# Dealing the expert slots over the SBUF partitions: neighbouring slots of each 32 stand four partitions apart

## The reference, cut to what matters

```python
def hier_moe(x, w_rg, w_re, w_g, w_u, w_d):
    ...
    ids = g_idx[:, None] * E_PER_GROUP + top_i.astype(jnp.int32)
    wts = (g_w * top_w).astype(x.dtype)
    return expert_dispatch(t, ids, wts, w_g, w_u, w_d).reshape(shp)
# for each expert e and the tokens xb that chose it:
    hb = jax.nn.silu(xb @ w_gate[e]) * (xb @ w_up[e])
    return (hb @ w_down[e]) * wb[:, None]
```

```
layer 0: 26 22 62 31 36 31 48 66 31 26 24 22 18 31 13 17 47 49 28 50 51 53 40 32 36 48 37 43 34 21 34 45
layer 1: 23 12 31 16 15 23 16 30 81 57 65 86 45 24 88 28 38 54 39 33 26 66 41 29 28 18 26 15 21 31 35 12
```

## Time and profile before

| | us |
|---|---|
| Median of 3 runs | 1980.47 |
| Lowest and highest run | 1979.82, 1981.99 |
| Span of the profiled execution, first to last instruction | 1975.5 |
| Median less span | 5.0 |

### The profile page before, as it was taken

How to read it: one execution, slowest core, us unless ns; L and a number is a source line. 1 busy time by engine, 2 the same in 40 slices (tenths; PEclk the granted TensorE clock), 3 DMA queues, 4 the chain that set the end, 5 groups by cost and what they waited for, 6 DMA issues and landing times.

```text
span 1975.5 us, 32588 instructions
## 1 busy us (share of the span) xinstructions
PE 1654.4 (84%) x12810; PEld 790.5 (40%) x12810; DVE 643.1 (33%) x1305; ACT 330.3 (17%) x752; POOL 216.5 (11%) x356
## 2 busy tenths in 40 slices
PE   6999888888889787887778879998968788778885
PEld 3444355554445322322223347764442222223232
DVE  3213467777612500000000068984160000000005
ACT  2000244434402100000000020004020000000001
POOL 1001122223200100000000012000020000000000
PEclk9999889988889799999998979999979999999997
DMA  9999378989963799999999989804169999999995
GB/s 373 324 369 347 142 278 311 338 327 349 367 239 125 290 420 427 416 427 424 427 410 429 422 295 302 283 10 171 43 239 425 426 415 428 425 427 427 425 422 202
DMA packets 99924, 659.09 MB, mean 334 GB/s; under 512 B 15147, under 2 KB 15148, under 8 KB 69706
## 3 DMA queue, kind: packets, MB, share of 16 engines
q1 hardware_dynamic: 70906, 569.76, 72.5%
q0 software_dynamic: 28896, 87.65, 12.0%
HBM read 643.08 MB, written 96.53 MB: 374 GB/s over the span
## 4 chain that ended last, share of the span: by engine, by line
PE 54%; DMA 34%; DVE 6%; issue 3%; ACT 2%; SPq 1%; POOL 0%; DVEq 0%; POOLq 0%; ACTq 0%
DMA ring<-in 33%; PE ps L2059 14%; PE ps L1706 9%; PE ps L2014 7%; PE ps L2222 6%; PE ps L1665 4%; PE ps L1828 2%; PE ps L2243 2%; PE ps L2079 1%; PE ps L1768 1%; DMA ring<-y_rows 1%; PE ps L1893 1%; PE ps L1744 1%; PE ps L1813 1%; DVE ring L1185 1%
## 5 line engine op out<-in xcount | busy, mean ns | idle before, releaser
L2059 PE MATMUL ps<-ring,big 128*32 128x512 f32 (+1 forms) x2688 | 476.9, 652 | 139.0 <-DMA ring<-in 133.0
L2059 PEld LDWEIGHTS ps<-ring,big 128*32 128x32 f32 (+1 forms) x2688 | 150.9, 132 | 460.6 <-issue 390.6
L1382 DVE TENSOR_TENSOR big<-big,ps 128x512 f32<-128x512 f32 x32 | 22.0, 688 | 828.7 <-PE ps L2059 783.3
L2079 PE MATMUL ps<-ring,big 128*32 128x512 f32 (+1 forms) x928 | 212.3, 594 | 17.0 <-ACT big L748 12.3
L748 ACT ACTIVATE big<-ps 128x512 f32<-128x512 f32 (+4 forms) x136 | 74.4, 548 | 739.7 <-PE ps L1665 415.2
L1706 PE MATMUL ps<-ring,act_t 128*128 128x512 f32 (+1 forms) x480 | 189.8, 594 | 0.6 <-DMA ring<-in 0.6
L2014 PE MATMUL ps<-ring,big 128*128 128x512 f32 (+1 forms) x288 | 123.0, 609 | 5.7 <-ACT big L1085 4.8
L2222 PE MATMUL ps<-act_t,ring 128*128 128x288 f32 x512 | 124.4, 406 | 0.0
L1706 PEld LDWEIGHTS ps<-ring,act_t 128*128 128x128 f32 (+1 forms) x480 | 78.0, 179 | 97.2 <-issue 96.2
L2079 PE MATMUL ps<-act_t,big 128*32 128x512 f32 (+1 forms) x416 | 99.0, 594 | 14.8 <-ACT big L748 11.5
L2222 PEld LDWEIGHTS ps<-act_t,ring 128*128 128x128 f32 x512 | 97.2, 190 | 26.8
(11 more groups left out here) (292 smaller groups left out, 1616.7 us busy)
## 6 DMA issues: line engine op xcount, KB each, us to landing
ring<-in SPq DMA_DIRECT2D x180, 2048.0 KB, 21.4
out<-in SPq DMA_DIRECT2D x16, 4080.0 KB
ring<-in SPq DMA_DIRECT2D x128, 256.0 KB, 8.2
ring<-in POOLq DMA_DIRECT2D x128, 256.0 KB, 8.2
act_t<-in SPq DMA_DIRECT2D x16, 2048.0 KB
ring<-in SPq DMA_DIRECT2D x28, 1024.0 KB, 9.3
ring<-in SPq DMA_DIRECT2D x24, 512.0 KB, 4.9
ring<-in POOLq DMA_DIRECT2D x24, 512.0 KB, 4.7
```

What stands on the lines that cost most here:

```text
L2059: ins = mm(ps[half, i, :], XgT[:, par_, k, half], slot(eslots(w)[i], 8)[:, k, :], start=(k == 0), stop=(k == KC - 1))
L2079: ins = mm(ps[half, 5 + h, :], hbT[:, k, half], down_weights(w, odd)[:, k, h * 512:(h + 1) * 512], start=(k == 0), stop=(k == 3))
```

## The change

The constants get two new tensors, `slot_at` (128 columns) and `rank_at` (64 columns), 192 columns or 96 KB more in `cst`. Partition m of a block holds no longer slot m, but slot 32*(m//32) + 8*(m%4) + (m%32)//4: slots stay in their group of 32 partitions, and there slots 0 to 7 stand on partitions 0, 4, 8, ... 28, slots 8 to 15 on 1, 5, ... 29, and so on. The two comparisons that make the one-hots read the new constants. The gathers, scatters, matmuls and waits are those of before, in number, shape and order, with other indices in them.

```diff
@@ -108,6 +108,10 @@
     c["count_up"] = np.broadcast_to(np.arange(P, dtype=f), (P, P)).astype(f)
+    m = np.arange(P)
+    slot_at = 32 * (m // 32) + 8 * (m % 4) + m % 32 // 4
+    c["slot_at"] = np.broadcast_to(slot_at.astype(f), (P, P)).astype(f)
+    c["rank_at"] = np.broadcast_to(1 + slot_at[0:HB].astype(f), (P, HB)).astype(f)
@@ -1440,7 +1444,7 @@
             V.tensor_tensor(unit0, rank0.unsqueeze(3).broadcast_to((P, NT, 2, HB)),
-                            C("count_up")[:, 1:HB + 1].unsqueeze(1).unsqueeze(1).broadcast_to((P, NT, 2, HB)),
+                            C("rank_at").unsqueeze(1).unsqueeze(1).broadcast_to((P, NT, 2, HB)),
                             ALU.is_equal).then_inc(r_table, 1)
@@ -1506,7 +1510,7 @@
             V.tensor_tensor(in_block, lo.unsqueeze(2).broadcast_to((P, NS, P)),
-                            C("count_up").unsqueeze(1).broadcast_to((P, NS, P)), ALU.is_equal).then_inc(r_table, 1)
+                            C("slot_at").unsqueeze(1).broadcast_to((P, NS, P)), ALU.is_equal).then_inc(r_table, 1)
```

## The result

| | before | changed |
|---|---|---|
| Median, us | 1980.74 (4 runs, 1979.82 to 1981.99) | 1970.82 (4 runs, 1968.66 to 1974.18) |
| Ratio, 95% interval | | 0.9946 (0.9932 to 0.9960) |
| Time and span of the profiled execution, us | span 1975.5 | 1970.49, span 1968.3 |

The direction is the forecast's, the size is not. Of the changed kernel the time and the span of one and the same execution are known: 2.2 us lie between them, not the 5.0 us taken for before. If it is 2.2 us before the change too, the profiled execution of before was about 2.8 us quicker than the median it was set against. The forecast does not hang on that: 1980.5 less 5.7 us is 1974.8 either way.

What follows compares the result with a forecast made beforehand. Weight loads keep the DMA queues full in the experts' stretches, so the engine with most token rows binds, with PE a fifth spare. 7.3 - 0.4 - 1.0 - 0.2 = 5.7 us less, giving 1974.8 us; range 1971.2 to 1979.5.

Steps and rivals of the forecast that it cites:

- the 0.153 us priced from bytes and rate: Gathers and scatters: a 4 KB token row costs its DMA engine 4096 B / 26.8 GB/s = 0.153 us.
- theory G: Follow-up, experts over both halves: the block-by-block sum of heaviest counts matters, not the heaviest total; about 4 us under the change.
- theory E: Follow-up, gathers: neighbouring descriptors on one engine cost, not its row count; half dealing brings half the gain or less.
- The 5.2 us of layer 0: Experts of layer 0: heaviest engine has 17 fewer rows, in gathers and scatters, 34 x 0.153 = 5.2 us saved.
- the 2.1 us of layer 1: Experts of layer 1: 7 fewer rows counted in gathers and 7 in scatters, 14 x 0.153 = 2.1 us saved.
- engines nearly level: Experts' stretches: the slowest of several close engines is later than one alone; 0.5 us a layer, 1.0 us lost.
- the small packets: Gathers and scatters: where the engine lost a row it gets a very small packet; 0.4 us lost, ends 0 to 0.8.
- 0.2 for the constants: Start, ahead of the first weight load: 96 KB more at 429 GB/s costs 0.2 us on the path.
- Runs scatter by 1 us: Range of the forecast: 1 us of scatter moves its low end from 1972.2 to 1971.2 us.
- 1 (only part arrives): Experts' stretches: the loop issue, landing, PE holds the heavy engine; half the gain, 1977.0 to 1978 us; chance 0.11.
- 2 (the change does not do it): Indirect transfers shared among engines otherwise than inferred, so only the constants count; 1980.7 us; chance 0.08.
- 3 (the eighth engine is slow): Experts' stretches: the eighth engine, slower by itself, gets more rows; 11.3 us more, 1991.9 us; chance 0.05.

Runs made afterwards that it cites:

- experiment 8: Changed kernel with each expert's slots spread over both halves of the partitions, matmuls in four column groups of 32; 1971.71 us (0.9967 of before), again 1975.54 us (0.9985).
- seventh experiment: Kernel before, with the gathers of blocks 1 to 15 in layer 1 moving no row (out of bounds); 1969.24 us against 1978.06, ratio 0.9952.
- layer 1 only: Changed kernel with slots dealt in layer 1 alone, layer 0 as before; 1979.22 us against 1978.50 before, ratio 0.9997.
- two apart: Changed kernel with half the dealing: two neighbouring slots stay on an engine, then the next engine follows; 1975.02 us against 1979.38 before, ratio 0.9977.
- layer 0 only: Changed kernel with slots dealt in layer 0 alone, layer 1 as before; 1973.67 us against 1978.50 before, ratio 0.9975.
- changed, second: The changed kernel measured again, no edit; 1971.21 us against 1979.38 before, ratio 0.9957.
- changed, third: The changed kernel measured once more, no edit; 1973.85 us against 1978.06 before, ratio 0.9978.
- odd groups reversed: Changed kernel, but in the second and fourth group of 32 partitions dealing begins at the last engine of the eight; 1971.59 us against 1978.50 before, ratio 0.9971.
- experiment 2: Changed kernel with slots reversed in each group of 32 (partition 31 - m%32), the heap on the eighth engine; 1980.38 us against 1979.38 before, ratio 1.0000.
- experiment 1: Changed kernel with the new constants loaded but both one-hots comparing with count_up, slots as before; 1979.15 us against 1979.38 before, ratio 1.0002.

## Why the prediction was right and where it was wrong

All traces but the two of experiment 8, cut at the comparison, and by the finer measure ("14 landings"). "Rows" are those that the heaviest engine moves fewer than before in a layer's full stretch (in the seventh experiment all 97, to the whole layer).

| kernel | before the experts | layer 0 | layer 1 | 14 landings, layer 0 / 1 | rows, layer 0 / 1 |
|---|---|---|---|---|---|
| before | 648.8 | 801.8 | 524.9 | 404.26 / 400.82 | 0 / 0 |
| constants only | 652.6 | 800.8 | 526.0 | 403.83 / 400.92 | 0 / 0 |
| reversed | 649.2 | 801.4 | 526.6 | 403.07 / 401.27 | 0 / 0 |
| layer 1 only | 652.2 | 802.1 | 522.4 | 404.63 / 398.75 | 0 / 14 |
| no gathered rows in layer 1 | 652.4 | 802.3 | 512.6 | 404.60 / 389.49 | 0 / 97 |
| two apart | 653.2 | 798.5 | 524.8 | 401.53 / 399.79 | 22 / 8 |
| layer 0 only | 646.6 | 797.2 | 525.9 | 399.09 / 400.35 | 34 / 0 |
| changed | 650.2 | 795.3 | 522.8 | 398.45 / 398.83 | 34 / 14 |
| changed, second | 647.5 | 797.4 | 524.7 | 398.92 / 398.76 | 34 / 14 |
| changed, third | 655.4 | 794.8 | 523.0 | 398.07 / 398.96 | 34 / 14 |
| odd groups reversed | 651.0 | 795.9 | 522.7 | 399.29 / 399.19 | 38 / 22 |

**The bound and the mechanism: right for the change.** With no rows less, layer 0 takes 801.7 us in the mean of five traces and layer 1 525.9 us of four. With 22, 34 and 38 rows less layer 0 takes 3.2, 5.5 (mean of four) and 5.8 us less; with 8, 14, 22 and 97 rows less layer 1 takes 1.1, 2.6 (mean of four), 3.2 and 13.3 us less. That is 34.7 us for 235 rows, 0.148 us a row, against the 0.153 us priced from bytes and rate. Five of the seven figures are single traces, and the layer 0 of one and the same kernel differs by up to 2.6 us between traces. The finer measure scatters less, by 0.2 us over the four traces dealt in layer 1 and by 1.0 us over the four dealt in layer 0. By it the change's 34 and 14 rows bring 5.4 and 2.0 us, 0.156 us a row. The other doses fall short of 0.153 us a row: two apart brings 3.6 us for 30 rows, the seventh experiment 11.4 us for 89, and the odd groups reversed bring 6.4 us for 60. Counting the heaviest engine block by block and adding up, as theory G does, gives the odd groups the rows of the change, 34 and 14, and fits them better. So the rows of the busiest engine are the cause, and its total over a layer prices them only roughly.

**Two more rivals.** *Another sharing of the partitions.* Counted from the same slots, eight neighbouring partitions to an engine would have the change save 0 rows in layer 0 and 4 in layer 1, two neighbouring ones in turn over all 16 engines 14 and 8, four neighbouring ones in turn over all 16 engines 3 and 15. The gains of 5.4 and 2.0 us fit none of these, and fit 34 and 14. *Neighbouring slots on one engine (theory E).* Layer 1 has as many pairs of neighbouring slots on an engine as layer 0, 852 each by the counts, and the change parts them all. By theory E both layers would gain alike; they gain 5.4 and 2.0 us. Whatever put the heap on an engine, its number of rows set the time (experiment 2), and the constants cost nothing that can be seen (experiment 1).

**Where the rows go: right.** The 5.2 us of layer 0 measured 5.5, the 2.1 us of layer 1 2.6 us. Together that is 8.1 us, 0.8 us over the 7.3. Most of the 0.8 us lies ahead of the full stretch: block 0's gather, which runs alone, lands 0.3 to 0.4 us sooner in each layer when its slots are dealt. In the chain of waits it is, before and changed, layer 0 and layer 1:

```profile
653.29 3.50 DMA big<-h_rows,sti
...
1455.03 3.38 DMA big<-h_rows,sti
```

```profile
654.72 3.19 DMA big<-h_rows,sti
...
1449.97 3.00 DMA big<-h_rows,sti
```

The prediction counted that gather at nothing.

**The step that failed first: the deductions.** From 7.3 us it took 1.0 for "engines nearly level", 0.4 for the small packets and 0.2 for the constants. The 1.4 us of the first two should show in the layers, which leaves 5.9 us. The layers measure 8.1 us together, and the experts' stretches alone 7.5 us: none of the 1.4 us appears. A misfit of 0.4 us in a single period was taken for a toll on every block, and for the changed kernel there is none that can be seen. For the odd groups, with engines more level still, there may be one: by the finer measure they gain 1.0 us less than the change, with 12 rows fewer. The 0.2 us for the constants lie ahead of the experts and are too small for the runs of experiment 1 (0.9991 to 1.0014) to tell.

**The step that failed second: the range.** "Runs scatter by 1 us" was read from three runs. In the experiments the kernel before ran 34, 35 and 26 times: medians 1979.38, 1978.50 and 1978.06, from 1971 to 1987 us. The table shows one source: the part ahead of the experts takes 646.6 to 655.4 us, with the same code in it but for the constants. So the median of before that the forecast started from lay 1.1 to 2.4 us above these, and the ratio of the first comparison is the most favourable of three (10.7, 8.5, 4.4 us). Whether some of that is a difference between chips is open. 7.9 us, their mean, agrees with the 8.1 us of the stretches; 5.7 us was too little by 2.4 us, and the rest of the distance to 9.9 us is scatter that the range should have held. With 3 us of scatter in place of 1 us the low end would have been about 1969 us, an estimate. (The stated end also has a slip: 1980.5 less 8.1 us, plus 0.2 for the constants, less 0.2 for rounding, is 1972.4 and not 1972.2.)

**The rivals.** 1 (only part arrives) is out for the change, where the full price arrives. With 89 to 97 rows gone eight to nine tenths of it arrive. 2 (the change does not do it) is out. 3 (the eighth engine is slow) is out by the reversed kernel: with 110 and 101 rows on that engine the time is that of before, ratio 1.0000. The Trainium skill, DMA: Bandwidth & Descriptors, section Latency and other measured facts, calls engines 7 and 15 usually slower; the runs here, on the partitions that it gives to 7, show no such handicap; engine 15 was not tried.

## What to carry to other kernels

Where plain loads kept all DMA engines busy, as here (share 1.01), the indirect transfers cost the rows of the busiest engine and not the mean. Find the filled partitions, count them by engine and block, and price a 4 KB row at 0.15 us on the engine that has most. Expect less than that once the engines are nearly level or many rows go at once. Slots that fill from the front heap on the same engines in each block, and a constant in the one-hot that places them deals them out at no cost that could be measured. Take a gross term whole when it fits the measured periods. Take the scatter of a median from many runs, or read the stretch that the change touches out of each trace.

## What the runs showed of the hardware that was not expected

A gather of 48 rows, with no other transfer under way, landed in 3.1 to 3.3 us (five dealt traces) and not in 3.4 to 3.5 us (five undealt) when neighbouring slots went to different engines, though the busiest engine had four rows in both cases. The 16 arrivals of one weight load lay up to 11.6 us apart while the mean DMA share was 1.01. A kernel with 14 and 34 rows fewer on its busiest engine than the change, and all its expert matmuls in column groups of 32, was no faster, in two measurements.
